# A streaming-encoder block on one core: the left-hand SBUF buffers move by 96 bytes

## What is computed

```python
h   = rms_norm(x, norm1_g);  z = h @ w_in
mix = concat(pool_mixer(z_pool), forgetting_attention(z_q, z_k, z_v, log_f)) @ w_out
x   = x + mix
ht  = rms_norm(x, norm2_g)
q   = (ht @ w_query).reshape(T, 8, 2, 128)
v1, i1 = top_k(q[:, :, 0] @ keys0.T, 16);  v2, i2 = top_k(q[:, :, 1] @ keys1.T, 16)
top_s, top_pos = top_k(all 256 sums v1 + v2, 16);  expert = i1 * 128 + i2 at top_pos
gates = softmax(top_s)
y = sum over heads and k of gates * gelu(expert_u[expert] . ht) * expert_v[expert]
x = x + y
```

## Time and profile before

| | us |
|---|---|
| median of 3 runs | 1440.74 |
| lowest and highest | 1440.31, 1441.36 |
| span of the profiled execution | 1439.4 |
| tensor engine busy | 1432.6 |
| VectorE, GpSimd, ScalarE busy | 1131.8, 977.5, 574.6 |
| DMA, mean over the span | 265 GB/s |

### The profile page before, as it was taken

How to read it: one execution, slowest core, us unless ns; L and a number is a source line. 1 busy time by engine, 2 the same in 40 slices (tenths; PEclk the granted TensorE clock), 3 DMA queues, 4 the chain that set the end, 5 groups by cost and what they waited for, 6 DMA issues and landing times.

```text
span 1439.4 us, 20447 instructions
## 1 busy us (share of the span) xinstructions
PE 1432.6 (100%) x7551; PEld 1278.1 (89%) x7551; DVE 1131.8 (79%) x1876; ACT 574.6 (40%) x799; POOL 977.5 (68%) x533
## 2 busy tenths in 40 slices
PE   9999999999999999999999999999999999999998
PEld 7766798899999999999999999888888888888887
DVE  6688551669999999699999995498777777777775
ACT  6775453333333333444444444333333333333332
POOL 3431544346888888866666675598887888878883
PEclk9999999999999999999999999999999999999999
DMA  6221233225787878989999986999888888888883
GB/s 227 103 88 45 103 110 102 89 99 177 257 262 261 276 271 271 346 285 362 357 357 363 365 298 228 366 386 351 343 346 345 328 328 344 345 343 324 332 302 117
DMA packets 122293, 381.57 MB, mean 265 GB/s; under 512 B 11768, under 2 KB 28280, under 8 KB 122240
## 3 DMA queue, kind: packets, MB, share of 16 engines
q1 hardware_dynamic: 70384, 202.69, 39.3%
q0 software_dynamic: 36864, 134.23, 25.4%
q10 hardware_dynamic: 14992, 44.06, 7.8%
HBM read 336.89 MB, written 44.06 MB: 265 GB/s over the span
## 4 chain that ended last, share of the span: by engine, by line
PE 98%; DVE 1%; ACT 1%; issue 0%; DVEq 0%
PE bank L744 29%; PE bank L745 28%; PE bank L746 28%; PE bank L1000 6%; PE bank L932 1%; PE bank L880 1%; PE bank L903 1%; PE wide L892 1%; PE bank L777 0%; PE bank L811 0%; PE wide L811 0%; PE bank L867 0%; PE bank L818 0%; PE wide L822 0%; PE wide L818 0%; PE bank L822 0%
## 5 line engine op out<-in xcount | busy, mean ns | idle before, releaser
L480 POOL TENSOR_TENSOR wl<-raw,wh 128x1024 fp32r<-128x1024 f32 x208 | 507.9, 2443 | 278.3 <-ACT wh L510 275.4
L744 PE MATMUL bank<-hh,wh 128*128 128x384 f32 (+1 forms) x1184 | 416.2, 352 | 0.2 <-DVE hl L1247 0.2
L745 PE MATMUL bank<-hl,wh 128*128 128x384 f32 (+1 forms) x1184 | 406.4, 343 | 0.0
L746 PE MATMUL bank<-hh,wl 128*128 128x384 f32 (+1 forms) x1184 | 406.4, 343 | 0.0
L744 PE MATMUL bank<-wh,Wh 128*128 128x512 f32 x768 | 299.0, 389 | 0.0
L746 PE MATMUL bank<-wh,Wl 128*128 128x512 f32 x768 | 298.8, 389 | 0.0
L745 PE MATMUL bank<-wl,Wh 128*128 128x512 f32 x768 | 298.8, 389 | 0.0
L510 ACT ACTIVATE wh<-raw 128x1024 fp32r<-128x1024 f32 (+1 forms) x217 | 227.8, 1050 | 141.4 <-PE bank L746 135.8
L744 PEld LDWEIGHTS bank<-hh,wh 128*128 128x128 f32 x1184 | 222.8, 188 | 7.9 <-DVE hl L1247 0.6
L745 PEld LDWEIGHTS bank<-hl,wh 128*128 128x128 f32 x1184 | 222.8, 188 | 7.1 <-issue 0.2
L746 PEld LDWEIGHTS bank<-hh,wl 128*128 128x128 f32 x1184 | 222.3, 188 | 7.6
(11 more groups left out here) (200 smaller groups left out, 1629.4 us busy)
## 6 DMA issues: line engine op xcount, KB each, us to landing
raw<-uT_dram SPq DMA_DIRECT2D x128, 512.0 KB
xraw<-v_dram SPq DMA_DIRECT2D x72, 512.0 KB
raw<-v_dram SPq DMA_DIRECT2D x56, 512.0 KB
a_dram<-act_a ACTq DMA_DIRECT2D x64, 384.0 KB
wf<-a_dram SPq DMA_DIRECT2D x32, 768.0 KB, 6.9
raw<-wst_dram SPq DMA_DIRECT2D x40, 512.0 KB
gates_dram<-gbuf ACTq DMA_DIRECT2D x32, 512.0 KB
gt<-gates_dram SPq DMA_DIRECT2D x32, 512.0 KB
```

Of the source, the lines that this page charges most:

```text
L480: pool.tensor_tensor(wl[:, n % SPLIT, :], raw_of(n), wh[:, n % SPLIT, :].bitcast(F32), ALU.subtract).then_inc(w_lo, 1)
L744: pe.matmul(dst, ah, bh, start=start, stop=False)
L745: pe.matmul(dst, ah, bl, start=False, stop=False)
L746: return pe.matmul(dst, al, bh, start=False, stop=stop)
```

## The change

Nothing is computed in another way. The constants lose one column (`C_EPS`, which held 1.0; the logarithm's bias reads a column of ones instead), and a filler `to_line` is allocated behind them, so that `keys` and all the left-hand buffers after it move up by 96 bytes and begin at 5120, a multiple of 512. `blockr` becomes a second name of `identr`; `pad`, whose rows aren't a multiple of 512 bytes, goes behind `wp`, and `slotT` loses what it doesn't use. The right-hand buffers stay.

```diff
-C_ID, C_MASK, C_IOTA, C_BLOCK, C_ONES, C_CNT, C_EPS = 0, 128, 256, 384, 512, 640, 704
-N_CONST = 705
+LINE = 512
+LEFT_EDGE = 2176
+C_ID, C_MASK, C_IOTA, C_BLOCK, C_ONES, C_CNT = 0, 128, 256, 384, 512, 640
+N_CONST = 704
...
         cst = sb("cst", [P, N_CONST])
+        sb("to_line", [P, (-LEFT_EDGE // 4 - N_CONST) % (LINE // 4)])
         keys = sb("keys", [P, 2, NKEY])
...
-        blockr = sb("blockr", [P, P], F32R, mixers)
-        pad = sb("pad", [P, 3, PAD + T], where=mixers)
+        blockr = identr
         pm = sb("pm", [P, T], where=mixers)
         newt = sb("newt", [P, T], where=mixers)
+        wp = sb("wp", [P, 4, P], where=mixers)
+        pad = sb("pad", [P, 3, PAD + T], where=mixers)
         rcol = sb("rcol", [P, TB], where=mixers)
         rrec = sb("rrec", [P, TB, 2], where=mixers)
-        wp = sb("wp", [P, 4, P], where=mixers)
...
-        slotT = sb("slotT", [P, 3, T], where=gates)
+        slotT = sb("slotT", [P, 2, DT], where=gates)
...
-                        act.activation(fg[:, 1, :], fg[:, 1, :], ACT.Ln, bias=cst[0:HEADS, C_EPS:C_EPS + 1])\
+                        act.activation(fg[:, 1, :], fg[:, 1, :], ACT.Ln, bias=cst[0:HEADS, C_ONES:C_ONES + 1])\
...
-    c[:, C_EPS] = 1.0
```

## The result

The changed kernel takes 1453.1 us (1452.85 to 1453.55) beside 1440.7 us: 1.0085 of the time before, 95% interval 1.0073 to 1.0097. It is 12.4 us slower; the forecast was no change, 1440.7 us within 1438.3 to 1443.1. The profiled execution has a span of 1450.9 us, 11.5 us more than before.

What follows compares the result with a forecast made beforehand. The prediction took the tensor engine, busy 1432.6 of 1439.4 us, as the bound. Tensor, chain and start terms of 0 left the span at 1439.4 us; with 1.3 us to the median, 1440.7 us, range 1438.3 to 1443.1.

Steps and rivals of the forecast that it cites:

- tensor-engine term: Large matmul groups: moved operand starts leave the pace unchanged, 0 us, bounded by 79 us gained or lost.
- rival 1: Large matmuls pay for straddled 512-byte lines; faster, 1434.5 us (moving operand) or 1409 us (weight load); chance 0.07.
- the fixed part depends on both addresses together: Matmul time beyond its columns, some 13.5 ns, depends on both operands' addresses; named as what would make the prediction wrong, unsized.
- Rival 3: Buffer addresses: some phases differ from those worked out, but all earlier phases price the same; 1440.7 us, chance 0.04.
- bound from below: Large matmul groups: at worst 79 us lost, only if a start could double the fixed part of each matmul.
- One cycle of 2.4 GHz per matmul: Large matmul groups: 0.42 ns on each of 5856 matmuls, 2.4 us, used to widen the range either way.
- two unchanged cases: Whole kernel: the forecast itself and Rival 3, both 1440.7 us, together given 0.88.
- the chain and the start: Early short VectorE/ScalarE steps and first weight landing: each 0 us, within 0.3 us either way.
- Rival 2: Gate stage: slower VectorE one-hot instructions make the tensor engine wait; 1447 to 1460 us, chance 0.04.

Runs made afterwards that it cites:

- m32: `tidy` with three gaps of 32 bytes, ahead of `hh`, `Wh1` and `Wh0`, which set stationary and moving operands 32 bytes apart; 1460.2 us.
- both512: The changed kernel with the right-hand buffers moved down by 416 bytes, so left and right all start on multiples of 512; 1440.9 us.
- tidy: The changed kernel with a filler of 32 bytes instead of 128, so every left-hand buffer starts where it did before the change; 1440.8 us.
- w1_back: The changed kernel with `Wh1` and `Wl1` alone moved down by 416 bytes, onto multiples of 512; 1450.3 us.
- m64: `tidy` with three gaps of 64 bytes, ahead of `hh`, `Wh1` and `Wh0`, which set stationary and moving operands 64 bytes apart; 1460.6 us.
- up448: The changed kernel with 448 columns instead of 384 in every matmul of the up stage, operand distance still 96; 1543.4 us.

## Why the prediction was wrong

**The step that failed is the tensor-engine term**, where the prediction took "0, the row nearest being 416 against 448". It measured some 12 us in the profiled executions (8.3 in the down stage, 2.7 in the query stage, 1.2 in the output projection). What carried the 0 was the phase of the right-hand buffers, called "an estimate from the sizes": 448. It is 416. So the comparisons of the earlier trace rows between left and right, which were read as two phases with one pace, compared a phase with itself. No pair of the large groups in the kernel before had a distance other than 0, and the sentence that moving by 32 bytes "changes nothing" had no row behind it. `m32` shows 6.5 ns for it. The trace could not have told; the program could, since every buffer's address is fixed when it is compiled.

**The question was also put too narrowly.** The prediction priced the phase of each operand by itself. Of rival 1 both readings fell: `both512` has every operand on a line and no gain. The one sentence that fitted stood under what would make it wrong, that "the fixed part depends on both addresses together", and it had no chance of its own. Rival 3 named the right edge, but its "all phases of before price the same" is the same error again. The bound from below, "by the same size lost only if a start could double the fixed part, for which no row speaks", left out the case that two starts which agreed until now would cease to: the change moves one side against the other, and that alone was a reason to give a loss more than 0.05.

**The unit of the price.** One cycle of 2.4 GHz per matmul, 2.4 us in all, set the width of the range. In the changed kernel the down stage pays 6.67 ns and the output projection 7.5 ns, 16 and 18 such cycles, on part of the matmuls. The two unchanged cases also have 0.89 by their own terms (0.85 and 0.04), not 0.88, which changes nothing else.

**What held.** The sum's structure held: after 200 us the tensor engine has no gap in either kernel, so its pace is the time. The other terms held too. VectorE's line 1404 and ScalarE's line 510 (1407 and 513 after the change) keep their durations of the earlier trace rows:

```profile
L1407 DVE TENSOR_TENSOR oh<-bank,slotT x96: 1218/1225/1227, 599.9 to 882.1; 128x1024 f32<-128x1024 f32 x96
L513 ACT ACTIVATE wh<-raw x217: 616/1052/1068, 6.2 to 1430.6; 128x1024 fp32r<-128x1024 f32 x108, 128x512 fp32r<-128x512 f32 x1
```

In the first 136 us the change gains 0.5 us at most, in the sense of the 0.3 + 0.3 us that were kept for the chain and the start. Rival 2 didn't occur: the one-hot matmuls begin and end 3.4 us later, and VectorE still waits for the tensor engine there (9.1 us in 10 waits).

**Lines, ports and beats.** The 16-byte lines of the Trainium skill (SBUF — State Buffer, Specifications) would give 0 for this change; the time rose by 12.4 us, and the cost found has a period of 256 bytes. The same page of the Trainium skill (Who interferes with whom) states that TensorE has two independent read ports, one for the moving operand and one for the weight load, and that it never waits on anyone. Read as a promise that it doesn't matter where the two operands lie, this differs from the measurement, which decides: a distance of 96 bytes between them lengthens a matmul of 512 columns by 6.7 ns. Of the beats that the Trainium skill (DMA: Bandwidth & Descriptors, How a descriptor splits into AXI transactions) counts for unaligned rows nothing showed: the share of the queue that carries the loads is 40.0% in `tidy`, where the starts are off a multiple of 256, and 39.7% in `both512`, where they are on one, not 4% less. The kernel before, with the starts of `tidy`, has 39.3%, so a difference of this size is that of single executions.

What is shown is that with 512 columns the distance of the starts modulo 256 sets the pace. That the cause is a collision of the two streams in the memory, which read at once, is argued from it only: no run took the overlap of load and matmul away. Nor do the runs tell whether the stationary operand that counts is the one being loaded or the matmul's own, since within a stage both start at the same phase.

## What to carry to other kernels

Where the tensor engine has no gaps and every float32r matmul of 384 or 512 columns loads its own weights, keep the starts of the stationary and the moving operand equal modulo 256 bytes, on both sides of the memory and in both slots of a double buffer; an aligned address by itself gave nothing here. With 448 columns equal starts weren't the best case. Before a change that moves buffers, read the addresses of both operands from the compiled program, and compare pairs, not single buffers. And a stage whose pace was measured once may have a second steady pace at the same addresses: with a wait added ahead of it, in one run, it lost 5.5 us beyond the later start.

## What the runs showed of the hardware

- The time from one float32r matmul's start to the next, each with its own weight load, at the 2.4 GHz level: 226.7 ns for 512 columns and 173.3 ns for 384, both columns x 0.417 ns + 13.3 ns, where the operands' starts are equal modulo 256. With 512 columns 32, 64, 96 and 128 bytes between them cost 5.6 to 6.7 ns more in the down stage, mean over both slots, and 96 bytes 7.5 ns in the output projection; 256 and 96 + 256 behave as 0 and 96.
- With 384 columns the same distance costs 0 or 3.33 ns (96 bytes: changed kernel and `w1_back`, each stable for over 1600 matmuls; 64 bytes: `m64`, before and from the gate stage on), by how the stretch is entered. In the down stage the slow pace outlives its cause by eight matmuls.
- 448 and 480 columns cost 2.5 and 3 ns beyond the rate at distance 0. At distance 96, 448 columns cost 6.7 ns by single starts before the gate stage (`up448`) and nothing from it on.
